# A hybrid decoder trunk on one core: the first squares wait for the rows alone, the position bias's trip through memory begins first, and TensorE multiplies zeros until its first factors

## What is computed

```
hn = RMSNorm(h)                       # x * rsqrt(mean(x*x) + 1e-6) * gain
z  = hn @ W_in                        # GLA | pool | sparse attention | gMLP columns
score  = relu(q_idx . k_idx) @ w_idx  # indexer: chooses 64 of the visible keys
bias   = rel_bias[rel_bucket(t - s)]  # 32 buckets x 4 heads, by distance
logits = q . k / 8 + bias             # over the chosen keys
h += [o_gla | o_pool | o_sparse | o_gmlp] @ W_out ;  h += cross_attn ;  h += ffn
```

## Time and profile before

| | |
|---|---|
| median of 3 runs | 1367.27 us (1364.92 to 1367.72) |
| the profiled execution, its own time | 1365.22 us |
| its span, first to last instruction | 1363.4 us |
| busy: PE, DVE, ACT, POOL | 1254.3 us (92%), 487.4 (36%), 370.1 (27%), 84.9 (6%) |
| mean granted TensorE clock | 0.998 |
| HBM read | 433.94 MB, 319 GB/s over the span |

### The profile page before, as it was taken

How to read it: one execution, slowest core, us unless ns; L and a number is a source line. 1 busy time by engine, 2 the same in 40 slices (tenths; PEclk the granted TensorE clock), 3 DMA queues, 4 the chain that set the end, 5 groups by cost and what they waited for, 6 DMA issues and landing times.

```text
span 1363.4 us, 15394 instructions
## 1 busy us (share of the span) xinstructions
PE 1254.3 (92%) x6158; PEld 760.4 (56%) x6158; DVE 487.4 (36%) x823; ACT 370.1 (27%) x563; POOL 84.9 (6%) x69
## 2 busy tenths in 40 slices
PE   6899999999999999999979779779779788999996
PEld 5768888888888687434324224224224225788432
DVE  1737377777654735301001001001001005988102
ACT  2433344444323414111001001001001005776102
POOL 0570000000007400000000000000000000000000
PEclk9999999999999999999999999999999999999999
DMA  9622614542282129899999999999999999999895
GB/s 359 284 93 97 238 68 152 219 186 93 88 344 93 63 97 406 346 415 427 428 427 429 429 427 428 430 428 428 429 429 427 428 430 427 428 427 399 362 427 248
DMA packets 37683, 435.73 MB, mean 320 GB/s; under 512 B 5820, under 2 KB 7936, under 8 KB 9600
## 3 DMA queue, kind: packets, MB, share of 16 engines
q1 hardware_dynamic: 37440, 434.48, 77.0%
q0 software_dynamic: 192, 0.53, 0.1%
HBM read 433.94 MB, written 1.05 MB: 319 GB/s over the span
## 4 chain that ended last, share of the span: by engine, by line
PE 61%; DMA 34%; DVE 2%; ACT 2%; issue 1%; SPq 0%; DVEq 0%; POOL 0%; ACTq 0%; POOLq 0%
DMA ring<-in_experts 32%; PE bank L2133 10%; PE bank L2213 9%; PE bank L1633 7%; PE bank L2016 6%; PE bank L1638 5%; PE bank L2143 5%; PE bank L1656 4%; PE bank L2020 3%; PE bank L1906 1%; PE bank L1913 1%; PE bank L1907 1%; PE bank L2066 1%; PE bank L2091 1%; PE bank L1615 1%
## 5 line engine op out<-in xcount | busy, mean ns | idle before, releaser
L2133 PE MATMUL bank<-ring,xs 128*64 128x512 f32 x1552 | 352.0, 596 | 41.4 <-DMA ring<-in_experts 41.4
L2133 PEld LDWEIGHTS bank<-ring,xs 128*64 128x64 f32 x1552 | 109.6, 137 | 248.2 <-issue 228.6
L2143 PE MATMUL bank<-ring,s_act 128*64 128x512 f32 x768 | 176.3, 597 | 34.4 <-DMA ring<-in_experts 34.2
L1520 DVE TENSOR_TENSOR s_act<-wsT,bank 128x256 f32<-128x256 f32 x49 | 20.6, 421 | 510.9 <-ACT wsT L935 510.9
L2143 PEld LDWEIGHTS bank<-ring,s_act 128*64 128x64 f32 x768 | 55.6, 136 | 142.7 <-issue 131.3
L2016 PE MATMUL bank<-x_both,wf_hi 128*128 128x512 f32 x336 | 118.9, 396 | 0.0
L935 ACT ACTIVATE wsT<-bank 128x256 f32<-128x256 f32 x49 | 18.8, 384 | 336.4 <-PE bank L2091 336.4
L1544 DVE TENSOR_TENSOR ring_lo<-ring,w_hi 128x2048 fp32r<-128x2048 f32 (+1 forms) x44 | 95.8, 2193 | 18.7 <-ACT w_hi L992 18.5
L870 ACT ACTIVATE wf_hi<-ring 128x1024 fp32r<-128x1024 f32 x66 | 69.8, 1059 | 98.5 <-PE bank L2016 67.2
L1633 PE MATMUL bank<-xnT,ring 128*128 128x256 f32 (+1 forms) x416 | 95.0, 388 | 1.1 <-DVE xnT L1106 1.1
L2020 PE MATMUL bank<-x_both,wf_lo 128*128 128x256 f32 x336 | 94.2, 280 | 0.0
(11 more groups left out here) (361 smaller groups left out, 1432.9 us busy)
## 6 DMA issues: line engine op xcount, KB each, us to landing
ring<-in_experts SPq DMA_DIRECT2D x166, 2048.0 KB, 29.1
ring<-in_packed SPq DMA_DIRECT2D x18, 1536.0 KB, 6.8
ring<-in_packed SPq DMA_DIRECT2D x11, 2048.0 KB, 12.1
ring<-in_packed SPq DMA_DIRECT2D x18, 1024.0 KB, 5.0
extra<-in_experts SPq DMA_DIRECT2D x2, 2048.0 KB, 12.7
ring<-in_packed SPq DMA_DIRECT2D x2, 1312.0 KB, 7.6
h<-in_x SPq DMA_DIRECT2D x2, 512.0 KB, 4.3
xnT<-in_xT SPq DMA_DIRECT2D x1, 1024.0 KB, 7.2
```

The source lines that it names most:

```text
L2133: i = mm(ps[d % 2][SMALL * side:SMALL * side + SMALL, :], xs[:, k, :], weights(u)[:, at:at + FC], start=k == 0, stop=k == KT - 1)
L2143: i = mm(ps[6 + half][SMALL * side:SMALL * side + SMALL, :], s_act[:, d % 4, x + side, :], weights(u)[:, at:at + FC], start=d == 0 and x = ...
```

## The change

Nothing is computed differently. Six things are moved or added to the program:

- ACT no longer waits for `loaded_first` before its table load and first squares; that wait now stands in front of `kiT`.
- SP issues the one-hot table and `rel_bias` before `xT` and `U_QI`, not after the parameters; `flip` goes behind `U_A` and counts under `loaded_mem`, which goes to 80.
- PE makes the bias's small product before its first factors, and waits for `loaded_const` (32) there.
- ACT copies the bias row before `kiT`.
- PE waits for `loaded_mem` before the flips.
- PE multiplies zeros twelve times (128x128 by 128x256) into bank 1 at its start, as soon as POOL has set `zeros`.

```diff
@@ sync engine
             sp.dma_start(columns[:, :, :], A["columns"]).then_inc(S["loaded_first"], 16)
+            sp.dma_start(gla[0:BUCKETS, 0:384], onehot).then_inc(S["loaded_const"], 16)
+            sp.dma_start(kdec[0:BUCKETS, 0:HEADS], A["rel_bias"]).then_inc(S["loaded_const"], 16)
             sp.dma_start(xnT[:, :, :], A["xT"]).then_inc(S["loaded_xT"], 16)
...
-                            sp.dma_start(gla[0:BUCKETS, 0:384], onehot).then_inc(S["loaded_const"], 16)
-                            sp.dma_start(kdec[0:BUCKETS, 0:HEADS], A["rel_bias"]).then_inc(S["loaded_const"], 16)
-                            sp.dma_start(glab[:, 0:P], flip).then_inc(S["loaded_const"], 16)
...
                     if s == U_A:
                         if layer < 1:
+                            sp.dma_start(glab[:, 0:P], flip).then_inc(S["loaded_mem"], 16)
@@ gpsimd, scalar (two places)
-            gp.wait_ge(S["loaded_mem"], 64)
+            gp.wait_ge(S["loaded_mem"], 80)
@@ scalar
             act.wait_ge(S["zeroed"], 1)
-            act.wait_ge(S["loaded_first"], 32)
...
                 norm(0, R_MIX)
+                if layer < 1:
+                    act.wait_ge(S["bias_ps"], 1)
+                    act.activation(gla[0:HEADS, 512:896], ps[7][0:HEADS, 0:384], ACT.Copy).then_inc(S["bias_row"], 1)
+                    act.wait_ge(S["loaded_first"], 32)
                 group("ki")
...
-                if layer < 1:
-                    act.wait_ge(S["bias_ps"], 1)
-                    act.activation(gla[0:HEADS, 512:896], ps[7][0:HEADS, 0:384], ACT.Copy).then_inc(S["bias_row"], 1)
@@ tensor
+            pe.wait_ge(S["zeroed"], 1)
+            for _ in range(12):
+                mm(ps[1][:, 0:256], zeros[:, 0:P], zeros[:, :], start=True, stop=True)
             pe.wait_ge(S["loaded_first"], 32)
             pe.wait_ge(S["loaded_h"], 32)
...
                 if layer < 1:
+                    pe.wait_ge(S["loaded_const"], 32)
+                    mm(ps[7][0:HEADS, 0:384], kdec[0:BUCKETS, 0:HEADS], gla[0:BUCKETS, 0:384], start=True, stop=True)\
+                        .then_inc(S["bias_ps"], 1)
                     factors_on_columns(layer, norm_no(layer, 0), 0)
...
-                if layer < 1:
-
-                    pe.wait_ge(S["loaded_const"], 48)
-                    mm(ps[7][0:HEADS, 0:384], kdec[0:BUCKETS, 0:HEADS], gla[0:BUCKETS, 0:384], start=True, stop=True)\
-                        .then_inc(S["bias_ps"], 1)
...
                     pe.wait_ge(S["bias_hank"], 32)
+                    pe.wait_ge(S["loaded_mem"], 80)
```

More of the change, by code:

```diff
@@ L770, in _ @@
                 if layer < 1:
-                    act.wait_ge(S["loaded_mem"], 64)
+                    act.wait_ge(S["loaded_mem"], 80)
                     for t in range(TT):
```

## The result

The changed kernel takes 1358.93 us in the median (1358.71 to 1359.27, 4 runs) against 1367.49 us for the kernel before (1364.92 to 1368.18, 4 runs): a ratio of 0.9945, with a 95% interval of 0.9928 to 0.9961, so faster by 0.4 to 0.7%. The profiled executions are 1359.27 and 1365.22 us, spans 1357.5 and 1363.4, which is 5.95 us apart. The medians are 8.56 us apart. Both numbers have to be explained.

The account below looks back on a forecast made before the run. PE (61% of the span) and experts' weight transfers (34%) bound the kernel, with two opening stretches not bound by PE. +0.1 - 0.80 - 3.12 - 1.66 + 0 = -5.5 us against 1365.22 gives 1359.7, range 1356.0 to 1363.5.

Parts of the forecast that it names:

- the case with 0.92: Whole kernel: faster by more than about 0.2%, 2.7 us; chance 0.50 + 0.33 + 0.09 = 0.92.
- the wait: PE's idle time before the flips, waiting for the bias's trip, goes: -3.12 us.
- the flips: The four flip matmuls run at the full clock, 1.74 us in place of 3.40: -1.66 us.
- the product: The bias's product leaves PE's busy stretch and costs nothing in its new place: -0.80 us.
- The read-back's landing: End of the bias's trip through memory: begun near 12 us, lands near 29, before PE asks near 43.
- The start term: Start of PE's first real product, waiting for `U_QI`: taken +0.1 us, between -0.2 and +0.95.
- The clock at the start: PE's first group of matmuls, slow start priced at 2.7 us: term between 0 and -2.7, taken 0.
- The chosen case: Clock falls again in PE's 2.8 to 3.4 us gap before the first real product: 0 us, chance 0.50.
- The clip: DVE's second choice starts only 3.8 us earlier, 1.7 less than PE; hidden by ACT's wait at `kT`: 0 us.

Follow-up runs that it names:

- e3_trip_alone: The kernel before with the bias's trip put first alone, no zeros, ACT waiting as before: 1360.94 us against 1366.52, ratio 0.9961.
- e5_zeros_alone: The kernel before with only the twelve products of zeros added at PE's start: 1362.27 us against 1366.52, ratio 0.9974.
- e1_no_zeros: The changed kernel without its twelve products of zeros: 1360.06 us, ratio 0.9949 against the kernel before.
- e6_unit_a_first: The changed kernel with `U_A` issued before the 852 KB of constants: 1358.79 us, ratio 0.9936 against the kernel before.
- e4_wait_alone: The kernel before with only ACT's wait for `loaded_first` moved to before `kiT`: 1367.27 us against 1366.52, ratio 1.0.

## Why the prediction was right

**Direction and size.** Forecast 1359.7, measured 1358.93; inside the range, and faster was the case with 0.92. The mechanism that I put first is the one found: `e3_trip_alone` gives 5.6 us by itself, against a sum of -5.5 with the wait, the flips and the product as its terms. In the profiled pair these three came out within 0.2 us each. The read-back's landing was forecast near 29 and came at 27.2. That the number is so close is luck in part: the opening gave 2.25 us more than the sum, and 1.8 us were lost behind it, neither of which the prediction had. For the median it named 1361.8, which is 2.9 us above what was measured.

**The start term was mis-sized.** "Taken +0.1, near the lower end because data, not issue, is what `U_QI` waits for" should have been -1.08 in this pair. I took one landing, 12.9, as fixed; fourteen traces have it anywhere between 11.9 and 13.0. And because `U_QI` and the factors were within 0.2 us of each other, I wrote that ACT's earlier squares buy at most 0.2. Two releasers that are level in one trace are not level in the next. In `e5_zeros_alone` `U_QI` landed 0.7 us earlier, and in `e3_trip_alone` the gains landed 0.6 us later; in both the factors came last, and in the second the wait was worth 1.2 us (against `e1_no_zeros`). SP's two extra issues cost nothing that shows, as forecast: `U_QI` is issued at 4.12 and not at 3.18, and lands at 12.14.

**The clock at the start.** The chosen case, that it falls again before the first real product, is what the profiled execution shows; but my reason was poor. I expected a gap of 2.8 to 3.4 us, and it was 1.67. The zeros began at 2.3 rather than 1.4 us. And the first slow stretch, 5 us before, was 3.3 after, a gain of 1.1 us up to `U_A`'s first product, where the weights and PE were level (landing at 24.20, product at 24.25). The forecast of this term was two-valued, and the runs show a scatter: with the same program the clock fell at 12.0, 12.6 and 12.9, and in `e6_unit_a_first`, whose opening on PE is the same, not at all. The prediction also says that no row shows PE on zeros. The trace of before has one: the kernel already multiplies zeros in eight matmuls (L2050, at 540.7 us) with the clock up, though it does not show them raising it.

**The clip.** DVE's second choice and `kT` cost nothing that can be seen: PE has no wait between 43.49 and 94 us. Right.

**What reached the end.** "A microsecond won in the opening should reach the end whole" holds for every trace up to 500 us (7.75 at `ag`, 7.78 at 640). Behind it, 0.8 us went at the first wait for experts' weights: one transfer took 10.1 us in place of 8.9, and those behind it came later. In other traces the same place gave up to 0.6 us or took up to 0.6, so it scatters with the transfers; why a transfer takes longer was not tried. The transfers were issued as much earlier as the opening had won, so the path that the prediction gave them is right. Another 1.1 went in the last combination, by the clock. I also cited the 2.6 us wait before L2213, over which the clock had stayed up, as a row on the gap's side. Of twelve traces without zeros in that wait it fell in it or just after it in eight, at 1.4 to 1.6 us each. One trace had shown one side of a coin.

**Against the medians** the gain is 8.56 us, not 5.95, since the profiled execution before was a quick one. In the three groups the kernel before runs from 1362.17 to 1371.17, the change from 1357.57 to 1361.09. The change takes away a 3 us wait in which the clock falls, for 3.4 us from 46.0 in the profiled execution and for 6.8 us in `e4_wait_alone`. I read that as the reason for the narrower scatter. The runs of the parts speak for it, with `e3_trip_alone` (without the wait) within 1.7 us and `e4_wait_alone` (with it) within 5.7, but it was not tried by itself.

## What to carry to other kernels

Begin the longest chain of small transfers first, even if its consumer is far off. Here one product and a copy moved ahead of 24 products took a 3 us wait, and the slow flips behind it, off the path. Price a clock that can fall in an idle gap of 1 to 3 us as a chance, not as a yes or no from one trace: here it fell in eight of twelve over 2.6 us, and in three of fourteen over 1.2 us (the wait near 530 us). Products of zeros into a free bank, cut to the length of the wait, kept it up in both late waits in both traces that had them, while twelve too many (5.0 us) made PE's first real product 4.5 us late. When two releasers are level in one trace, cost the removal of either as anything up to their scatter.

## What was not expected of the hardware

- In the change's profiled execution the granted clock fell to half after 1.5 us of idle PE (10.51 to 12.0), and yet it stayed up over 2.0 and 2.6 us of idle in others (before L2213 and L2082 in the kernel before). The length of the gap alone doesn't decide.
- Products of zeros raise the clock as others do: 0.43 us apart up to 5.0 us in the change, 0.21 from 5.3 on. In `e5_zeros_alone` they were 0.43 apart up to 8.0 us, with the same start at 2.29.
- PE's first matmul came at 2.29 us although its `zeros` were there at 1.33; ACT's table load, released by the same memset, began at 1.44.
- A landing that nothing in the program touches, `U_QI`'s, moves by 0.8 us between eleven executions with the same order ahead of it (11.92 to 12.74).
